# The moving columns of 64 units read and written pair by pair, in 2 to 128 parts of the row

## The reference

```
x = x + 0.5 * swiglu(rmsnorm(x), ffn1 weights)          # 2048 -> 5632 -> 2048
h = rmsnorm(x);  z = h @ w_in                            # 2048 -> 6448 columns
o_hg  = gated linear recurrence on 4 x 1024 columns of z (8 heads)
o_nsa = sparse attention on the other columns (16 query heads, 2 kv heads:
        compressed, selected and window branches)
x = x + concat(o_hg, o_nsa) @ w_out                      # 2048 -> 2048
x = x + cross_attention(rmsnorm(x), rmsnorm(mem))        # wq, wk, wv: 2048 -> 512, wo: 512 -> 2048
x = x + 0.5 * swiglu(rmsnorm(x), ffn2 weights)
return rmsnorm(x)
```

## Time and profile before

| | |
|---|---|
| median of 3 runs | 2089.19 us (2088.74 to 2089.35) |
| the profiled execution, whole | 2089.34 us |
| its span, first to last instruction | 2087.5 us |
| TensorE matmuls busy | 98% of the span |
| TensorE weight loads busy | 82% |
| VectorE busy, ScalarE busy | 54%, 45% |
| the chain that ended last: TensorE | 96% |
| of it, the line of `unit` (L1350) | 89% |
| mean granted TensorE clock | 0.982 |
| rate of all DMA | 180 GB/s |

### The profile page before, as it was taken

How to read it: one execution, slowest core, us unless ns; L and a number is a source line. 1 busy time by engine, 2 the same in 40 slices (tenths; PEclk the granted TensorE clock), 3 DMA queues, 4 the chain that set the end, 5 groups by cost and what they waited for, 6 DMA issues and landing times.

```text
span 2087.5 us, 25300 instructions
## 1 busy us (share of the span) xinstructions
PE 2055.7 (98%) x9614; PEld 1713.4 (82%) x9614; DVE 1118.3 (54%) x1402; ACT 941.8 (45%) x1185; POOL 0.2 (0%) x4
## 2 busy tenths in 40 slices
PE   7999999999999999999989999999999999999997
PEld 6888888888888888788879888888888888888886
DVE  4454544454445455765684665655445454444444
ACT  5444444444444454544451554554444444444443
POOL 0000000000000000000000000000000000000000
PEclk9999999999999999999995999999999999999999
DMA  8666666666666656655510465466666666656653
GB/s 281 191 189 189 185 191 190 188 188 208 204 199 191 191 175 202 210 172 154 174 39 0 142 201 192 144 190 191 187 188 189 190 189 188 210 190 192 195 195 131
DMA packets 198822, 376.41 MB, mean 180 GB/s; under 512 B 13152, under 2 KB 19680, under 8 KB 198624
## 3 DMA queue, kind: packets, MB, share of 16 engines
q1 hardware_dynamic: 195984, 372.97, 59.1%
q10 hardware_dynamic: 2768, 2.48, 0.4%
HBM read 373.31 MB, written 2.10 MB: 180 GB/s over the span
## 4 chain that ended last, share of the span: by engine, by line
PE 96%; DVE 2%; ACT 1%; DMA 1%; issue 0%; DVEq 0%; SPq 0%; ACTq 0%
PE psum L1350 89%; PE psum L1361 2%; PE psum L1615 1%; PE psum L1569 1%; PE psum L1537 1%; PE psum L1550 0%; DVE att L1197 0%; DMA ident<-c_ident 0%; ACT w_hi L468 0%; DMA w_raw<-in_w_in 0%; DVE w_lo L838 0%; PE psum L1599 0%; PE psum L1646 0%; PE psum L1738 0%; PE psum L1516 0%
## 5 line engine op out<-in xcount | busy, mean ns | idle before, releaser
L838 DVE TENSOR_TENSOR w_lo<-w_raw,w_hi 128x1024 fp32r<-128x1024 f32 x696 | 850.8, 1224 | 894.2 <-ACT w_hi L468 892.9
L468 ACT ACTIVATE w_hi<-w_raw 128x1024 fp32r<-128x1024 f32 x696 | 736.8, 1060 | 1010.5 <-PE psum L1350 994.4
L1350 PE MATMUL psum<-w_hi,xT_hi 128*128 128x512 f32 (+1 forms) x1824 | 714.4, 392 | 11.8 <-DVE w_lo L838 8.7
L1350 PE MATMUL psum<-w_hi,xT_lo 128*128 128x512 f32 (+1 forms) x1824 | 709.4, 389 | 0.0
L1350 PE MATMUL psum<-w_lo,xT_hi 128*128 128x512 f32 (+1 forms) x1824 | 709.3, 389 | 0.0
L1350 PEld LDWEIGHTS psum<-w_hi,xT_hi 128*128 128x128 f32 x1824 | 343.7, 188 | 83.8 <-issue 10.2
L1350 PEld LDWEIGHTS psum<-w_hi,xT_lo 128*128 128x128 f32 x1824 | 343.7, 188 | 71.0
L1350 PEld LDWEIGHTS psum<-w_lo,xT_hi 128*128 128x128 f32 x1824 | 344.0, 189 | 68.8
L1350 PE MATMUL psum<-w_hi,ffT_hi 128*128 128x512 f32 x928 | 363.0, 391 | 0.0
L1350 PE MATMUL psum<-w_hi,ffT_lo 128*128 128x512 f32 x928 | 361.3, 389 | 0.0
L1350 PE MATMUL psum<-w_lo,ffT_hi 128*128 128x512 f32 x928 | 361.1, 389 | 0.0
(11 more groups left out here) (205 smaller groups left out, 677.5 us busy)
## 6 DMA issues: line engine op xcount, KB each, us to landing
w_raw<-in_g SPq DMA_DIRECT2D x176, 512.0 KB, 3.7
w_raw<-in_u SPq DMA_DIRECT2D x176, 512.0 KB, 3.7
w_raw<-in_d SPq DMA_DIRECT2D x176, 512.0 KB, 4.4
w_raw<-in_w_in SPq DMA_DIRECT2D x88, 512.0 KB, 4.4
w_raw<-in_w_out SPq DMA_DIRECT2D x32, 512.0 KB, 3.8
w_raw<-in_cw SPq DMA_DIRECT2D x8, 512.0 KB, 4.0
w_raw<-in_wk SPq DMA_DIRECT2D x8, 512.0 KB, 3.6
w_raw<-in_wq SPq DMA_DIRECT2D x8, 512.0 KB, 4.0
```

The costliest lines, as they stand in the source:

```text
L468: nc.scalar.activation(w_hi[:, slot], w_raw[:, slot], ACT.Copy).then_inc(w_hi_ready, 1)
L838: nc.vector.tensor_tensor(w_lo[:, slot], w_raw[:, slot], w_hi[:, slot].bitcast(F32), ALU.subtract)\
L1350: mm = nc.tensor.matmul(dst[:, t, 0:width], act_t, w[:, slot, kk, 0:width], start=(first and kk == 0 and n == 0), stop=(last and kk == KT_ ...
```

## The change

`unit` gets an argument `parts`. With `parts` at 1 it does what it did. With another number the 512 columns of both the moving operand and the output are seen as `parts` parts of equal length, and each part as a list of pairs. The walk takes the first pair of every part in turn, then the second pair of every part, and so on. Source and output are walked in the same order, so each column of the result still lands in its own place. The step from one pair to the next is the length of a part: with 2 parts 256 columns (1024 bytes), with 128 parts 4 columns (16 bytes). The pair itself is two neighbours of 4 bytes.

Each touched stage has its own number: 2, 4, 8 and 16 for `w_in`'s groups 0, 2, 3 and 4, then 32 for the keys, 64 for the queries, 128 for the values, and 2 for the output projection.

```diff
+PARTS = {0: 2, 2: 4, 3: 8, 4: 16}
+PARTS_K, PARTS_Q, PARTS_V, PARTS_O = 32, 64, 128, 2
...
-            def unit(u, slot, hi, khi, lo, klo, dst, width, first, last):
+            def unit(u, slot, hi, khi, lo, klo, dst, width, first, last, parts=1):
+
+                def columns(v):
+                    return v.rearrange("p (a b e) -> p b a e", a=parts, e=2) if parts > 1 else v
...
-                            mm = nc.tensor.matmul(dst[:, t, 0:width], act_t, w[:, slot, kk, 0:width],
+                            mm = nc.tensor.matmul(columns(dst[:, t, 0:width]), act_t, columns(w[:, slot, kk, 0:width]),
                                                   start=(first and kk == 0 and n == 0),
                                                   stop=(last and kk == KT_U - 1 and n == 2))
...
                     unit(u, u % SLOTS, xT_hi, 2 * j, xT_lo, 2 * j, pair[g % 2], IN_GROUPS[g][1],
-                         j == 0, j == U_G - 1)
+                         j == 0, j == U_G - 1, PARTS.get(g, 1))
```

More of the change, by code:

```diff
@@ L1688, in _ @@
                 u = U_MEMK + j
-                unit(u, u % SLOTS, ffT_hi, MEM_T + 2 * j, ffT_lo, MEM_T + 2 * j, pair[0], NW, j == 0, j == U_G - 1)
+                unit(u, u % SLOTS, ffT_hi, MEM_T + 2 * j, ffT_lo, MEM_T + 2 * j, pair[0], NW, j == 0, j == U_G - 1, PARTS_K)
                 if j == 3:
@@ L1697, in _ @@
                 u = U_XQ + j
-                unit(u, u % SLOTS, xT_hi, 2 * j, xT_lo, 2 * j, pair[1], NW, j == 0, j == U_G - 1)
+                unit(u, u % SLOTS, xT_hi, 2 * j, xT_lo, 2 * j, pair[1], NW, j == 0, j == U_G - 1, PARTS_Q)
                 if j == 1:
@@ L1704, in value_unit @@
                 u = U_MEMV + j
-                unit(u, u % SLOTS, ffT_hi, MEM_T + 2 * j, ffT_lo, MEM_T + 2 * j, pair[0], NW, j == 0, j == U_G - 1)
+                unit(u, u % SLOTS, ffT_hi, MEM_T + 2 * j, ffT_lo, MEM_T + 2 * j, pair[0], NW, j == 0, j == U_G - 1, PARTS_V)
             value_unit(0)
@@ L1758, in _ @@
                 unit(u, u % SLOTS, ffT_hi, OX + 2 * j, ffT_lo, OX + 2 * j, pair[(n + 1) % 2], NW,
-                     j == 0, j == U_XOG - 1)
+                     j == 0, j == U_XOG - 1, PARTS_O)
                 if j == U_XOG - 1 and n in (1, 2):
```

## The result

The changed kernel takes 2240.76 us (median of 4 runs, 2240.31 to 2242.16) against 2088.97 us before it. The ratio is 1.0727, with a 95% interval from 1.0714 to 1.074: it is 7.3% slower. The prediction said no change, 2089.2 us, and gave 2241 us to its rival A.

What follows compares the result with a forecast made beforehand. TensorE was taken to set the pace. Profiled 2089.34 us, removed 0, added 0, gave 2089.3 us, or 2089.2 against the runs' median. The range to hold 8 in 10 was 2081 to 2147 us.

Steps and rivals of the forecast that it cites:

- rival A: All 768 touched matmuls: every pair costs as much as four neighbours, starts 0.425 us apart, 152 us more, 2241 us; chance 0.17.
- What bounds the kernel: Whole kernel: TensorE, busy for 98% of the span, sets the pace; a nanosecond more on one matmul adds directly to run time.
- no instruction or wait would move: Touched stages: no instruction or wait added, removed or moved; loads, copies and evacuations keep their shapes; cost 0.
- The stage windows: Trace stretches read as the touched stages, such as group 2 of `w_in` from 793.71 to 815.24 us, giving 0.2266 us a matmul.
- the 0.85 us gap: Values' stage: the only gap in TensorE's work among the stages shown, 0.85 us, read as the wait for `vx`.
- the cost of the read: Moving operand in touched stages: 256 pieces of 8 bytes instead of one run of 2048 bytes, taken to cost 0.
- The write: Output into PSUM in touched stages: 256 pieces of 8 bytes, taken to cost 0, though no trace row bounded it from near.
- The upper bound of 0.198 us a matmul: Touched matmuls: feed or drain at half rate, 0.425 us as at half clock instead of 0.227, 152 us over 768.
- B: One to three touched stages: only some steps cost, pieces falling on the same bank; 19.0 us a stage; chance 0.13.
- the 0.0106 us that nothing accounted for: Each 512-column matmul: 0.2266 us against 0.216 for the float32 product, a difference that is not array time.
- the three rows that seemed to fit: Trace rows L1487, L1615 and L1190, walks in pieces; the first and last read as free, L1615 as open to a factor of two.

## Why the prediction was wrong

**What bounds the kernel** was right. TensorE sets the pace, nothing covered the loss, and nothing gave it back: 152.5 us in the stages, 151.0 in the span. That no instruction or wait would move was right too. The stage windows it was read from were 11 us off; the 0.85 us gap that the earlier trace rows seems to give to the values' stage lies behind it.

**The step that failed** is the cost of the read: "I take 0, by the rows nearest to it". It measured 0.10 to 0.26 us a matmul, 152.5 us in all. L1487 was misread. It takes every second of 128 columns, so 64 columns from 32 lines. 32 lines x 1.77 ns are 56.6 ns, and the measured distance for two was 57. I held the 57 against the array's 54 and called it a walk at full rate; both limits give about the same number there, because a plain float32 column keeps the array busy for twice as long as a column in `unit`. So the row couldn't tell them apart, if the two instructions that run side by side also read side by side, and each line once. That last part is argued: no run here varies the read of plain float32. L1615, with the steps of the values' stage, was rightly called open up to a factor of two; by the same count it visits 32 lines, some 57 ns, and its 110 ns would have hidden that. L1190 is another engine at a third of the pace (512 numbers in 681 to 687 ns, against 227), and says nothing about this limit.

**The write** at 0 was right by luck: nothing stood behind it.

**Rival A** had the place, the reason and the price. Its argument, that the 0.2266 us of the plain row are above the array's time, so that something beside the array is at its limit already, is what the runs bear out: 2 of every 4 columns, half of the array's work on the same 128 lines, take 226.6 ns too. It was given 0.17. The upper bound of 0.198 us a matmul is the mean of what was measured (152.5 / 768 = 0.1986), but not a bound: the single stages go from 0.10 (2 parts) to 0.26 us (8 parts). That one of the stages would differ for its step, as B said, was true on top of A. The cheaper stages are those with 2 parts. That A's 2241 us meets the measured 2240.76 is partly luck: its price is that of the array at the lower granted clock, and it lies between the cheap stages and the dear ones.

The Trainium skill's rule on SBUF in "Advanced Engine Details and Errata", Memory Cachelines, that two hits on a line of 16 bytes absorb the latency of the access, had been taken as agreeing with L1487. It does not hold for this moving operand at 2.4 GHz: two numbers of a line cost 1.77 ns, as much as four.

## What to carry to other kernels

Count the lines of 16 bytes that the moving operand visits, not its columns: for 4-byte data of this type most visits took 1.7 to 1.9 ns, less where a walk comes back to a line at once and 2.36 with one step. A matmul lasts as long as the larger of its array time and its visits, and pieces must be whole, aligned lines. The order of the output in PSUM is free down to pairs, so a permutation that is needed belongs on the output side, if the source can stay in order. And when a row of the trace seems to show that something is free, ask whether another limit has the same value there; the 0.0106 us that nothing accounted for told more than the three rows that seemed to fit.

## What the runs showed of the hardware that was not expected

- A plain row of 512 is itself at the limit of its read at full clock. It takes 226.6 ns. The array needs 213, half of the 427 that the same matmul takes at the granted clock of 0.50, and half of the columns from the same lines take 226.6 as well. Some 13 of these ns are there with 64 lines too.
- The pace of the read does not follow the granted clock: a walk took 567 ns at 1.00 and at 0.50.
- Coming back to a line soon costs less. With one other line between, a visit took 1.28 to 1.33 ns (pairs in 2 parts); with two between, 1.31 (shifted fours in 2 parts, 313 / 240) and 1.47 (pairs in 3 parts, 353 / 240); with three or more, 1.68 and above.
- A walk can have several steady speeds, 431 and 483 ns, or 440, 453 and 487, and changes between them where other work breaks the row. The cause is open; that it vanished with narrow stationary values in two stages points to the loads of stationary values, but isn't shown.
- A step of 24 columns costs 2.36 ns a visit, and fours from 32 parts, at 223 ns, a little less than the plain row. Fours with steps of 128 to 1024 bytes, all powers of two, took 247 to 278 ns. All three are open too.
